# One softmax step placed elsewhere in the expert stage of a two-layer decoder trunk, with two slots for its operand

## The chip, the cores and the metric

The kernel runs on 1 core of one Trainium2 chip. The time is the device time of one execution in microseconds (us), taken as the median of several runs. All data is float32.

## What is computed

Two layers work on 256 tokens of width 1024: layer 0 mixes tokens by gated linear attention, layer 1 by a gated delta rule. After each mixer comes an expert stage ("PEER"), the part that the change touches. Each of 8 heads picks 16 experts of 16,384 for each token by a product of two key tables:

```python
v1, i1 = lax.top_k(s1, PEER_TOPK)            # s1, s2: scores of 128 keys each
v2, i2 = lax.top_k(s2, PEER_TOPK)
cand = (v1[..., :, None] + v2[..., None, :]).reshape(n_tok, PEER_HEADS, PEER_TOPK * PEER_TOPK)
sc, pos = lax.top_k(cand, PEER_TOPK)         # idx: the experts that pos stands for
gate = jax.nn.softmax(sc, axis=-1).astype(h.dtype)
...
ue = jnp.take(u, ib, axis=0)                 # a row of 1024 numbers for each chosen expert
act = gb * jax.nn.gelu(jnp.einsum('nd,nkd->nk', tb, ue))
ve = jnp.take(v, ib, axis=0)
return jnp.einsum('nk,nkd->nd', act, ve)
```

## The kernel before

The expert stage is cut into four **stretches**: layer 0 with tokens 0 to 127 and 128 to 255, then layer 1 likewise (`w` = 0 to 3 in the code, stretches 1 to 4 in the text). A stretch has four **head pairs**, so there are 16 pairs, k = 0 to 15. A pair has 32 chosen experts for each of the 128 tokens (tokens lie on the partitions). One step s of a pair takes one expert for each token.

Each engine has a program of its own, and an engine works strictly in its order. Where two programs run on one engine (experts and mixer), the generator `interleave` merges them by the due times that each `yield` names; the times are written out by hand and decide the order only. The mixer of layer 1 runs beside stretches 2 and 3.

For a pair k the work is:

- **Routing** on VectorE (DVE), `routing(k)`: top 16 of the two score lists, of the 256 sums, then the indices `idx`, in 14 slices. Slices 1 to 14 of pair k + 1 lie behind the dots 11 to 24 of pair k (s = 10 to 23). Slice 9 writes the scores less their maximum into `ex`; slice 14 writes `idx` and `spread_i`. For the first pair of stretches 1, 3 and 4 (k = 0, 8, 12) routing stands as one block ahead of the pair's dots; pair 4, the first of stretch 2, is routed in pair 3.
- **Exponential** on ScalarE (ACT), `exp(k)`, in place in `ex`, then **softmax** on VectorE, `softmax(k)`: a sum, a reciprocal and a product, three small instructions, into `gate`.
- **Gathers** by GpSimd (POOL): from s = 0 on one indirect DMA of 128 rows of `u` for each step into one of 8 buffers `ub` (line 1961), behind `idx_ready`; gather n waits until dot n - 8 has run. Beside them run the gathers of `v` rows of the pair before (line 1972), 12 buffers.
- **Dots** on VectorE (line 1129), one for each step: the product of a gathered row with the token, summed.
- **Slot rows**: TensorE (PE) transposes `spread_i` (line 1582) into PSUM; VectorE makes from it the row numbers of the `v` gathers, `slot_rows(k)`, behind the ninth dot (s = 8).
- **Weights** behind the second dot of the next pair: gelu of the dots (ACT) times `gate`, transposed by TensorE, and products with the gathered `v` rows (line 1596) into the sum `y`.

At the end of a stretch VectorE adds the gated sum `y` to `x` (lines 1110 to 1114), for which ScalarE copies the gate rows (`gate_rows`, line 1335) out of PSUM. SyncE's queue streams weight blocks of 1 MB through three ring places (line 351); the next is issued when TensorE has used the block three before.

The lines before that the text speaks of:

```python
if p == w == 0:
    yield t0 - 42
    for i, _ in enumerate(routing(k)):
        yield t0 - 40 + 2 * i
    softmax(k)
...
if s == 8:
    slot_rows(k)
if s >= 10:
    next(ahead, None)
```

Of the kernel before, what the change touches and what calls it, by code (L numbers as in the profile page):

```python
# [19 lines left out]
P = 128  # L20
# [6 lines left out]
class Signal:  # L27
# [9 lines left out]
    def next(self):  # L37
        self.base += 1
        return self.base
# [39 lines left out]
def trunk_kernel(nc, x_in, c, ada_w, ada_b, norm_mix_g, norm_ffn_g, gla_w_in, gla_g1, gla_w_g2, gla_b_g2, gla_norm_g,  # L79
# [16 lines left out]
    with ctx:  # L96
# [674 lines left out]
        def decoder(scr):  # L771
# [7 lines left out]
            NL = len(LEVELS)  # L779

# [21 lines left out]
            best, ex = sb(scr, "best", [P, 2, TOPK]), sb(scr, "ex", [P, 2, TOPK])  # L802
# [4 lines left out]
            idx, idxf = sb(scr, "idx", [P, 2, SP_], U32), sb(scr, "idxf", [P, SP_])  # L807
            gate, dots = sb(scr, "gate", [P, 2, SP_]), sb(scr, "dots", [P, 2, SP_])
            spread_i, spread_a = sb(scr, "spread_i", [P, 4, SP_]), sb(scr, "spread_a", [P, 4, SP_])
            half4 = sb(scr, "half4", [P, 2 * SP_])  # L810
            idx4 = sb(scr, "idx4", [P, 2, SP_], U32)
# [152 lines left out]
            with nc.Block() as block:  # L964
# [18 lines left out]
                def _(dve):  # L983
# [4 lines left out]
                    def routing(k):  # L988
# [65 lines left out]
                        dve.tensor_tensor(by_head(idx[:, k % 2, :]), chosen[:, :, 0, :], chosen[:, :, 1, :], ALU.add).then_inc(idx_ready.sem, 1)  # L1054
# [3 lines left out]
                        dve.tensor_tensor(spread_i[:], idxf[:].unsqueeze(1).to_broadcast([P, 4, SP_]), mask4[:], ALU.mult).then_inc(idx_spread.sem, 1)  # L1058
                        yield

                    def softmax(k):
                        dve.wait_ge(exp_done.sem, exp_done.at(k + 1))
                        link(dve.tensor_reduce(total[:], ex[:], AX, ALU.add))
                        link(dve.reciprocal(total[:], total[:]))
                        dve.tensor_tensor(gate[:, k % 2, :].rearrange("p (h n) -> p h n", n=TOPK), ex[:],
                                          total[:].unsqueeze(2).to_broadcast([P, 2, TOPK]), ALU.mult).then_inc(gates_ready.sem, 1)

                    def slot_rows(k):
                        dve.wait_ge(idx_turned.sem, idx_turned.at(k + 1))
                        pairs = turned_idx.rearrange("p (n a) -> p n a", a=2)  # L1070
                        link(dve.tensor_copy(half4[:], pairs[:, :, 0]))
                        link(dve.tensor_tensor(half4[:], half4[:], pairs[:, :, 1], ALU.add))
# [11 lines left out]
                    def experts():  # L1084
# [4 lines left out]
                        for w in range(4):  # L1089
                            layer, t = w // 2, w % 2  # L1090
                            for p in range(PAIRS + 1):
# [33 lines left out]
                                for s in range(SP_):  # L1125
# [7 lines left out]
                                    if s == 8:  # L1133
                                        slot_rows(k)
# [900 lines left out]
```

## Time and profile before

| | |
|---|---|
| median of 3 runs | 1979.09 us (1977.34 to 1979.3) |
| span of the profiled execution | 2045.4 us, mean granted clock of TensorE 0.811 |
| PE / DVE / ACT / POOL busy | 74% / 56% / 19% / 52% of the span |
| moved by DMA | 703.86 MB, mean 344 GB/s |

The profiled execution has no time of its own beside its span, which runs from its first to its last instruction and is 66 us longer than the median; everything read from the trace is on this longer scale. "Busy" counts the time in instructions; idle time is put down to whatever released the engine. The granted clock is a share of 2.4 GHz.

### The profile page before, as it was taken

Reading aid. Unit: us, or ns where it says so; the run is one execution under the profiler, and the core shown is the slowest. Engines: PE = TensorE matmul, PEld = TensorE weight load, DVE = VectorE, ACT = ScalarE, POOL = GpSimd, SP = SyncE. Lnnn points to the kernel's source line nnn. Section 1 sums busy time; section 2 is a strip of 40 time slices with the busy share of each in tenths; the row PEclk is TensorE's granted clock in tenths of the full one; section 3 lists DMA queues with packets and bytes.
Section 4 is the critical chain, followed back from the end, with each engine's and each line's share of the span. In section 5 each row is a group of like instructions: output and inputs, shape, how many; then the busy total and the mean of one; then the engine's idle time right before and its main releaser. Section 6 shows DMA issues by size and latency. Waiting matters only on the chain.

```text
span 2045.4 us, 21763 instructions
## 1 busy us (share of the span) xinstructions
PE 1518.1 (74%) x8148; PEld 975.4 (48%) x8148; DVE 1153.2 (56%) x2731; ACT 390.4 (19%) x912; POOL 1065.9 (52%) x1031
## 2 busy tenths in 40 slices
PE   7998985777788668767887866877878751656656
PEld 6743882443443556656654465665655620000001
DVE  5454386555550878567443386858734448656430
ACT  1212110000000551451211164144121110000000
POOL 0000157766655565754564456465566365666664
PEclk8999976666667879989998878989899885667678
DMA  9453499999999998897999899799799988999997
GB/s 347 177 211 149 170 390 393 410 411 412 411 411 362 376 371 299 336 393 241 346 414 412 335 391 353 245 369 389 242 393 414 412 330 312 377 370 375 375 375 268
DMA packets 173113, 703.86 MB, mean 344 GB/s; under 512 B 23360, under 2 KB 23744, under 8 KB 155728
## 3 DMA queue, kind: packets, MB, share of 16 engines
q0 software_dynamic: 147456, 536.94, 69.1%
q1 hardware_dynamic: 25552, 165.53, 20.2%
q8 instruction: 65, 1.06, 0.2%
q14 instruction: 40, 0.33, 0.0%
HBM read 701.34 MB, written 1.05 MB: 343 GB/s over the span
## 4 chain that ended last, share of the span: by engine, by line
PE 24%; POOL 16%; DVE 16%; issue 14%; DMA 11%; another core or an unknown queue 5%; ACT 4%; POOLq 0%; SPq 0%; DVEq 0%; ACTq 0%
DMA ub<-in_peer_u,idx 8%; POOL ub L1961 7%; DVE ub L1129 7%; POOL vb L1972 6%; PE PS L1596 6%; PE PS L1704 3%; PE PS L1640 2%; POOL mods L1972 2%; PE PS L1927 2%; PE PS L1878 2%; DMA ring<-in_gdn_z 2%; DVE ring L1244 1%; PE PS L1657 1%; ACT ring L1418 1%
## 5 line engine op out<-in xcount | busy, mean ns | idle before, releaser
L1961 POOL DMA_INDIRECT ub<-in_peer_u,idx x512 | 540.9, 1056 | 413.2 <-DVE dots L1129 244.6
L1129 DVE CUSTOM_DVE_ANT_0 ub<-ub,h 128x1024 f32<-128x1024 f32 x384 | 464.2, 1223 | 219.9 <-DMA ub<-in_peer_u,idx 155.2
L1596 PE MATMUL PS<-vb,z 128*32 128x512 f32 x1348 | 395.7, 774 | 110.0 <-DMA vb<-in_peer_v,idx 62.4
L1972 POOL DMA_INDIRECT vb<-in_peer_v,idx x337 | 346.5, 1028 | 198.3 <-issue 94.8
L1596 PEld LDWEIGHTS PS<-vb,z 128*32 128x32 f32 x1348 | 64.5, 126 | 333.2 <-issue 187.8
L1129 DVE CUSTOM_DVE_ANT_0 ub<-ub,PS 128x1024 f32<-128x1024 f32 x128 | 154.0, 1218 | 100.3 <-DMA ub<-in_peer_u,idx 71.7
L1657 PEld LDWEIGHTS PS<-c_act,ring 128*128 128x128 f32 x896 | 139.8, 245 | 61.3 <-issue 61.2
L1657 PE MATMUL PS<-c_act,ring 128*128 128x1 f32 x896 | 141.0, 286 | 31.9 <-issue 31.6
L1596 PE MATMUL PS<-mods,z 128*32 128x512 f32 x444 | 138.0, 782 | 34.8 <-DMA mods<-in_peer_v,idx 25.9
L1972 POOL DMA_INDIRECT mods<-in_peer_v,idx x111 | 117.8, 1061 | 33.9 <-issue 33.9
L1704 PE MATMUL PS<-hT,ring 128*128 128x128 f32 x1024 | 127.1, 286 | 7.7 <-DMA ring<-in_gdn_qkv 7.6
L1704 PEld LDWEIGHTS PS<-hT,ring 128*128 128x128 f32 x1024 | 122.9, 201 | 16.2 <-DMA ring<-in_gdn_qkv 8.9
L1972 POOL DMA_INDIRECT ub<-in_peer_v,idx x64 | 59.9, 936 | 112.3 <-DVE dots L1129 48.3
L1946 POOL IOTA iota<- 128x16 f32 x1 | 0.1, 149 | 204.9 <-POOLq L408 204.9
L1575 PE MATMUL PS<-ident,spread_a 128*128 128x128 f32 x16 | 6.0, 378 | 107.2 <-issue 67.4
L1418 ACT ACTIVATE ring<-ring,taps 128x128 f32<-128x128 f32 x256 | 76.4, 387 | 0.3
L1927 PE MATMUL PS<-hT,ring 128*128 128x128 f32 x512 | 65.6, 292 | 10.0 <-ACT z L1321 10.0
L1301 ACT ACTIVATE ex<-ex 128x32 f32<-128x32 f32 x16 | 3.7, 229 | 356.8 <-DVE ex L1038 251.7
L1927 PEld LDWEIGHTS PS<-hT,ring 128*128 128x128 f32 x512 | 63.9, 208 | 16.2 <-ACT z L1321 10.5
L1878 PE MATMUL PS<-ring,hT 128*128 128x256 f32 x256 | 60.7, 396 | 12.5 <-DMA ring<-in_gdn_z 8.2
L1596 PEld LDWEIGHTS PS<-mods,z 128*32 128x32 f32 x444 | 22.6, 126 | 99.2 <-DMA mods<-in_peer_v,idx 63.2
L1897 PE MATMUL PS<-ring 128*128 128x256 f32 x256 | 59.7, 390 | 5.4 <-DMA ring<-in_gdn_w_out 5.2
(328 smaller groups left out, 2232.9 us busy)
## 6 DMA issues: line engine op xcount, KB each, us to landing
ring<-in_gdn_qkv SPq DMA_DIRECT2D x32, 1024.0 KB
ring<-in_ada_late SPq DMA_DIRECT2D x28, 1024.0 KB
ring<-in_peer_wq SPq DMA_DIRECT2D x24, 1024.0 KB
ring<-in_ada_w SPq DMA_DIRECT2D x10, 2048.0 KB, 8.2
ring<-in_gdn_z SPq DMA_DIRECT2D x16, 1024.0 KB
ring<-in_gdn_w_out SPq DMA_DIRECT2D x16, 1024.0 KB
ring<-in_gla_w_in SPq DMA_DIRECT2D x6, 2048.0 KB, 8.3
ub<-in_peer_u,idx POOLq DMA_INDIRECT x512
```

The costliest lines, as they stand in the source:

```text
L1129: dve.tensor_tensor_reduce(out=ub[:, n % UB, :], in0=ub[:, n % UB, :], in1=by_token, scale=1.0, scalar=0.0, op0=ALU.mult, op1=ALU.add, acc ...
L1244: dve.tensor_tensor(dst[:, vs, :], dst[:, vs, :], core.ps(name, lv, gq), ALU.add).then_inc(emptied["D"].sem, 1)
L1418: last = act.activation(tapped_by[:, j, c, :], here[:, c, j:j + P], ACT.Copy, scale=taps[:, j, 16 * hf + 4 * un + c:16 * hf + 4 * un + c + 1])
L1596: last = pe.matmul(y[32 * j:32 * j + 32, e, :], z[:, j, 28 * b:28 * b + 32], rows[:, e * 512:(e + 1) * 512], start=False, stop=False, skip ...
L1640: last = pe.matmul(PS[:, 3 + b % 2, c * S:(c + 1) * S], w[:, k, c * P:(c + 1) * P], hT[:, k, :], start=(k == 0), stop=(k == KD - 1))
L1657: last = pe.matmul(PS[:, 7, cols:cols + 1], w[:, k, c * P:(c + 1) * P], c_act[:, k:k + 1], start=(k == 0), stop=(k == KD - 1))
L1704: last = pe.matmul(PS[:, 3 + un, (2 * bb + c) * P:(2 * bb + c + 1) * P], w[:, k, c * P:(c + 1) * P], hTm[:, k, :], start=(k == 0), stop=(k ...
L1878: last = pe.matmul(ps, hTm[:, k, :], w[:, k, :], start=(k == 0), stop=(k == KD - 1))
L1897: last = pe.matmul(ps, oT[:, part * KD + k, :], w[:, k, :], start=(part == k == 0), stop=(part == 1 and k == KD - 1))
L1927: last = pe.matmul(PS[:, 3 + un % 2, (2 * bb + c) * P:(2 * bb + c + 1) * P], w[:, k, c * P:(c + 1) * P], hTm[:, k, :], start=(k == 0), sto ...
L1961: pool.indirect_dma_start(ub[:, n % UB, :], None, u_rows, off).then_inc(u_land[n % UB].sem, 16)
L1972: pool.indirect_dma_start(rows, None, v_rows, off).then_inc(land.sem, 16)
```

## The change

It does four things.

1. `softmax(k)` for k = 0, 8 and 12 no longer follows that pair's routing; it stands behind the sixth dot (s = 5) of the pair itself.
2. For the other 13 pairs `softmax` no longer stands behind the last dot of the pair before (s = 31) but behind its dot 26 (s = 25); their `exp` is due at 20/32 of the pair, where it was due at 22/32.
3. `ex` and `spread_i` get two slots, taken in turn. The wait on `exp_done` ahead of writing `ex` is gone, and the wait on `idx_turned` ahead of writing `spread_i` is for one pair earlier. `softmax` also waits on `gates_ready` of the softmax before it. `half4` is no longer a tile of its own but the first 64 columns of `fold`.
4. On ScalarE `exp(8)` and `exp(12)` stand ahead of the gate rows of the stretch that ends, where they stood behind them.

```diff
+            def routed_in(w, p):
+                k = w * PAIRS + p
+                return [(k + 1, 10)] if w == 0 or p < PAIRS - 1 else []
...
-            best, ex = sb(scr, "best", [P, 2, TOPK]), sb(scr, "ex", [P, 2, TOPK])
+            best, ex = sb(scr, "best", [P, 2, TOPK]), sb(scr, "ex", [P, 2, 2, TOPK])
...
-            half4 = sb(scr, "half4", [P, 2 * SP_])
+            half4 = fold[:, 0, 0:2 * SP_]
...
-                        if k:
-                            dve.wait_ge(exp_done.sem, exp_done.at(k))
-                        dve.tensor_tensor(ex[:], best[:], best[:, :, 0:1].to_broadcast([P, 2, TOPK]), ALU.subtract).then_inc(ex_ready.sem, 1)
+                        dve.tensor_tensor(ex[:, nth_routed[k] % 2], best[:], best[:, :, 0:1].to_broadcast([P, 2, TOPK]), ALU.subtract).then_inc(ex_ready.sem, 1)
...
-                        if k:
-                            dve.wait_ge(idx_turned.sem, idx_turned.at(k))
+                        if nth_routed[k] >= 2:
+                            dve.wait_ge(idx_turned.sem, idx_turned.at(nth_routed[k] - 1))
...
                     def softmax(k):
-                        dve.wait_ge(exp_done.sem, exp_done.at(k + 1))
-                        link(dve.tensor_reduce(total[:], ex[:], AX, ALU.add))
+                        mine = ex[:, nth_routed[k] % 2]
+                        dve.wait_ge(exp_done.sem, exp_done.at(nth_routed[k] + 1))
+                        if nth_routed[k]:
+                            dve.wait_ge(gates_ready.sem, gates_ready.at(nth_routed[k]))
+                        link(dve.tensor_reduce(total[:], mine, AX, ALU.add))
...
                                     for i, _ in enumerate(routing(k)):
                                         yield t0 - 40 + 2 * i
-                                    softmax(k)
...
                                             yield ROUTE_AT[w + 1] + 2 * i + 2
-                                        softmax(k)
...
+                                late = [k] if p == 0 and w != 1 else []
...
-                                    if s == 8:
-                                        slot_rows(k)
-                                    if s >= 10:
-                                        next(ahead, None)
-                                for _ in ahead:
-                                    pass
-                                if following is not None:
-                                    softmax(following)
+                                    for j in late if s == 5 else []:
+                                        softmax(j)
+                                    for j, _, after in turned_in(w, p):
+                                        if s == after:
+                                            slot_rows(j)
+                                    for steps_of, j, first in ahead:
+                                        if first <= s < first + 14:
+                                            next(steps_of)
+                                        if s == min(first + 15, SP_ - 1):
+                                            for _ in steps_of:
+                                                pass
+                                            softmax(j)
...
-                                if p < PAIRS - 1 or (w == 0 and p == PAIRS - 1):
-                                    yield t0 + span * 22 / SP_
-                                    exp(k + 1)
+                                for j, first in routed_in(w, p) if p < PAIRS else []:
+                                    yield t0 + span * (first + 10) / SP_
+                                    exp(j)
+                                if p == PAIRS and w + 1 in ROUTE_AT:
+                                    yield ROUTE_AT[w + 1] + 21
+                                    exp(k)
                                 if p == PAIRS:
                                     yield t0 + span * 25 / SP_
                                     gate_rows((1, 3, 5, 6)[w], w % 2)
-                                if p == PAIRS and w + 1 in ROUTE_AT:
-                                    yield ROUTE_AT[w + 1] + 21
-                                    exp(k)
```

`turned_in(w, p)` gives slot rows the place that they had (s = 8), and `nth_routed[k]` is k. The orders of TensorE, GpSimd and SyncE are the same as before, instruction for instruction.

The first place is VectorE at the first pair. In the rows, `ISA ub,dots` with the `ISA dots` behind it is one dot, and `total` and `gate` are softmax. Before, behind the routing of pair 0:

```order
L1055 TENSOR_TENSOR idxf<-chosen 128x32
L1058 TENSOR_TENSOR spread_i<-idxf,mask 128x128
L1063 TENSOR_REDUCE total<-ex 128x2
L1064 RECIPROCAL total<-total 128x2
L1065 TENSOR_TENSOR gate<-ex,total 128x32
L1129 ISA ub,dots<-ub,h 128x1024
L1129 ISA dots 128x1
L1129 ISA ub,dots<-ub,h 128x1024
```

After the change, from the sixth dot of pair 0 on; the five dots ahead of it follow `spread_i` directly:

```order
L1142 ISA ub,dots<-ub,h 128x1024
L1142 ISA dots 128x1
L1078 TENSOR_REDUCE total<-ex 128x2
L1079 RECIPROCAL total<-total 128x2
L1080 TENSOR_TENSOR gate<-ex,total 128x32
L1142 ISA ub,dots<-ub,h 128x1024
L1142 ISA dots 128x1
L1142 ISA ub,dots<-ub,h 128x1024
L1142 ISA dots 128x1
L1142 ISA ub,dots<-ub,h 128x1024
L1142 ISA dots 128x1
L1086 COPY fold<-PS 128x64
```

Softmax moved over six dots; three dots are left between it and the copy that begins slot rows.

The second place is VectorE at the border of pairs 0 and 1, which stands for the 13 pairs of point 2. Before, from dot 32 of pair 0 on:

```order
L1129 ISA ub,dots<-ub,h 128x1024
L1129 ISA dots 128x1
L1063 TENSOR_REDUCE total<-ex 128x2
L1064 RECIPROCAL total<-total 128x2
L1065 TENSOR_TENSOR gate<-ex,total 128x32
L1129 ISA ub,dots<-ub,h 128x1024
L1129 ISA dots 128x1
L1129 ISA ub,dots<-ub,h 128x1024
L1129 ISA dots 128x1
L1081 TENSOR_TENSOR gate<-dots,gate 128x32
L1082 TENSOR_TENSOR spread_a<-gate,mask 128x128
```

After, from dot 26 of pair 0 on:

```order
L1142 ISA ub,dots<-ub,h 128x1024
L1142 ISA dots 128x1
L1078 TENSOR_REDUCE total<-ex 128x2
L1079 RECIPROCAL total<-total 128x2
L1080 TENSOR_TENSOR gate<-ex,total 128x32
L1142 ISA ub,dots<-ub,h 128x1024
L1142 ISA dots 128x1
```

The three instructions of softmax stand six dots earlier, and dot 32 is followed by the next pair's dots.

The third place is ScalarE at the border of stretches 2 and 3, where `h<-PS` is the copy of the gate rows and `mods<-PS` the last two copies of scores. Before:

```order
L1528 ACTIVATE mods<-PS 128x512 x2
L1335 ACTIVATE h<-PS 128x1024
L1301 ACT_TABLE_LOAD
L1301 ACTIVATE ex<-ex 128x32
L1372 ACT_TABLE_LOAD
L1372 ACTIVATE nrs<-eps 128x1
```

After:

```order
L1546 ACTIVATE mods<-PS 128x512 x2
L1319 ACT_TABLE_LOAD
L1319 ACTIVATE ex<-ex 128x32
L1353 ACTIVATE h<-PS 128x1024
L1390 ACT_TABLE_LOAD
L1390 ACTIVATE nrs<-eps 128x1
```

The exponential and its table load moved ahead of the gate rows; the number of table loads is the same.

## Rows read from the trace of the kernel before

**Rows 1.** The page: part 1 by engine, and the DMA line of part 2 (40 slices).
```profile
PE 1518.1 (74%) x8148; PEld 975.4 (48%) x8148; DVE 1153.2 (56%) x2731; ACT 390.4 (19%) x912; POOL 1065.9 (52%) x1031
...
DMA  9453499999999998897999899799799988999997
```

**Rows 2.** One source line, L1063: count, durations, and what ended its waits.
```profile
L1063 DVE TENSOR_REDUCE total<-ex x16: 174/180/188, 256.5 to 1896.2; 128x2 f32<-128x32 f32 x16
...
  issue: 47.7, 2
  ACT ex L1301: 15.3, 1
```

**Rows 3.** Timeline of VectorE, first pair: start, duration, instruction, [idle before <- releaser].
```profile
240.93 0.29 DVE L1058 TENSOR_TENSOR spread_i<-idxf,mask 128x128 f32<-128x128 f32 x1
...
256.49 0.19 DVE L1063 TENSOR_REDUCE total<-ex 128x2 f32<-128x32 f32 x1 [15.27 <-ACT ex L1301]
...
257.02 1.22 DVE L1129 CUSTOM_DVE_ANT_0 ub<-ub,h 128x1024 f32<-128x1024 f32 x1
...
266.19 1.22 DVE L1129 CUSTOM_DVE_ANT_0 ub<-ub,h 128x1024 f32<-128x1024 f32 x1
...
271.88 0.22 DVE L1071 COPY half<-PS 128x64 f32<-128x64 f32 x1 [4.46 <-issue]
```

**Rows 4.** Timeline of TensorE at the end of the first score products.
```profile
269.72 2.01 PE L1630 MATMUL PS<-keysT,ring 128*128 128x128 f32 x16
271.57 0.27 PE L1582 MATMUL PS<-ident,spread_i 128*128 128x128 f32 x1
```

**Rows 5.** Timeline of GpSimd: gathers of key rows, first pair.
```profile
241.08 1.10 POOL L1961 DMA_INDIRECT ub<-in_peer_u,idx  x1 [34.75 <-DVE idx L1054]
...
258.52 1.68 POOL L1961 DMA_INDIRECT ub<-in_peer_u,idx  x1 [7.65 <-DVE dots L1129]
...
272.34 0.94 POOL L1961 DMA_INDIRECT ub<-in_peer_u,idx  x1 [0.30 <-issue]
```

**Rows 6.** Timeline of SyncE's queue: weight blocks, first pair.
```profile
238.72 8.13 SPq L351 DMA_DIRECT2D ring<-in_peer_wq  x2
254.32 47.58 SPq L351 DMA_DIRECT2D ring<-in_ada_late  x8
```

**Rows 7.** Busy time by stretch: PE, PEld, DVE, ACT, POOL, granted clock, DMA share, GB/s.
```profile
240.00:272.00 32.00, 32.00 (x172) 28.74 (x170) 12.10 (x27) 6.92 (x16) 19.01 (x16) 1.00 0.95 342
272.00:316.00 44.00, 29.54 (x158) 29.45 (x157) 43.18 (x115) 2.27 (x6) 26.07 (x24) 0.55 1.01 410
316.00:640.00 324.00, 245.42 (x1136) 130.29 (x1137) 164.47 (x404) 10.18 (x16) 216.45 (x212) 0.65 1.02 407
```

**Rows 8.** Timeline of VectorE at the border of stretches 2 and 3.
```profile
1161.49 0.19 DVE L1063 TENSOR_REDUCE total<-ex 128x2 f32<-128x32 f32 x1 [23.83 <-issue]
...
1166.51 0.69 DVE L1110 TENSOR_TENSOR h<-PS,h 128x512 f32<-128x512 f32 x1 [4.41 <-PE PS L1562]
...
1182.92 0.18 DVE L1162 TENSOR_TENSOR xa<-ab,dtb 128x16 f32<-128x16 f32 x1 [3.52 <-ACT ab L1382]
```

**Rows 9.** Timeline of ScalarE at the same border.
```profile
1152.85 0.60 ACT L1528 ACTIVATE mods<-PS 128x512 f32<-128x512 f32 x1 [0.85 <-remote]
1158.90 1.02 ACT L1335 ACTIVATE h<-PS 128x1024 f32<-128x1024 f32 x1 [5.45 <-PE PS L1610]
...
1161.23 0.23 ACT L1301 ACTIVATE ex<-ex 128x32 f32<-128x32 f32 x1
```

**Rows 10.** Timeline of ScalarE in stretch 3: one exponential behind the mixer's work.
```profile
1336.15 0.22 ACT L1301 ACTIVATE ex<-ex 128x32 f32<-128x32 f32 x1
```

**Rows 11.** Timeline of VectorE in stretch 3: the 27th dot of that pair, and the wait after dot 28.
```profile
1340.93 1.22 DVE L1129 CUSTOM_DVE_ANT_0 ub<-ub,h 128x1024 f32<-128x1024 f32 x1
...
1348.82 0.69 DVE L1184 TENSOR_TENSOR ring<-ring 128x512 f32<-128x512 f32 x1 [5.51 <-issue]
```

**Rows 12.** One source line, L1961: gathers of key rows, durations min/median/max.
```profile
L1961 POOL DMA_INDIRECT ub<-in_peer_u,idx x512: 932/937/1989, 241.1 to 1978.2; - x171
```

More of the change, by code:

```diff
@@ L779, in decoder, with turned_in @@
             NL = len(LEVELS)
+            IDX, IDX4 = 2, 2
+            ROUTED = list(range(4 * PAIRS))
+            nth_routed = {k: n for n, k in enumerate(ROUTED)}
+            def turned_in(w, p):
+                return [(w * PAIRS + p, 3, 8)]
+            def routed_in(w, p):
+                k = w * PAIRS + p
+                return [(k + 1, 10)] if w == 0 or p < PAIRS - 1 else []
             area = ring_flat[:, 3 * 2048:]
@@ L1073, in slot_rows @@
-                        quads = half4[:].rearrange("p (n a) -> p n a", a=2)
-                        dve.tensor_tensor(idx4[:, k % 2, :], quads[:, :, 0], quads[:, :, 1], ALU.add).then_inc(rows_ready.sem, 1)
+                        link(dve.tensor_copy(half4, pairs[:, :, 0]))
+                        link(dve.tensor_tensor(half4, half4, pairs[:, :, 1], ALU.add))
+                        quads = half4.rearrange("p (n a) -> p n a", a=2)
+                        dve.tensor_tensor(idx4[:, k % IDX4, :], quads[:, :, 0], quads[:, :, 1], ALU.add).then_inc(rows_ready.sem, 1)
@@ L1084, in experts @@
+                        dve.tensor_tensor(spread_a[:], gate[:, k % IDX, :].unsqueeze(1).to_broadcast([P, 4, SP_]), mask4[:], ALU.mult).then_inc(acts_ready.sem, 1)
                     def experts():
@@ L1115, in experts @@
                                     break
-                                following = k + 1 if p < PAIRS - 1 or w == 0 else None
-                                ahead = routing(following) if following is not None else iter(())
+                                ahead = [(routing(j), j, first) for j, first in routed_in(w, p)]
+                                late = [k] if p == 0 and w != 1 else []
                                 if layer and p == 0:
@@ L1566, in experts @@
                         pe.wait_ge(prepared.sem, prepared.at(1))
+                        turns = 0
                         for w in range(4):
@@ L1590, in experts @@
                                         yield t0 + span * (4 * b + 4) / SP_
+                                        if turning and turning[0][1] <= 4 * b + 4:
+                                            turning, turns = turn_rows()
                                         for e in range(2):
@@ L1606, in experts @@
                                             spread_gate(GATE_FFN[w // 2])
+                                while turning:
+                                    yield t0 + span * turning[0][1] / SP_
+                                    turning, turns = turn_rows()
                     def spread_gate(q):
```

54 lines of the change are left out of this document (29 added, 25 removed).

## Prediction

> **What bounds the kernel now.** I read the page first. No engine is busy all the time, but the DMA line stands at 9 tenths through most of the span [rows 1]. The table by stretch then says who rules at the place that the change touches: from 240 to 272 us TensorE is busy in all 32.00 us (the score products of layer 0), from 272 to 316 VectorE is busy in 43.18 of 44, and from 316 to 640 the DMA share is 1.02 at 407 GB/s while VectorE works 164 of 324 us [rows 7]. So stretch 1 is bound by TensorE, then VectorE, then DMA. Last I took the waits of softmax itself: 16 softmaxes, 15.3 us of wait for the exponential once, and 47.7 us in two others [rows 2]. All the rest ran without a wait. The change can only gain at these three places, and each must be followed to the next wait.
>
> **The start of stretch 1 (k = 0).** VectorE ends the routing with `spread_i` at 240.93 and stands until 256.49, since ScalarE does the exponential between copies that wait for score products; the first dot begins at 257.02 [rows 3]. The first gather was issued at 241.08 [rows 5]. The trace doesn't show how soon its row could be used. Bounds: not before the 1.10 us of the issue itself, and not later than the 7.67 us from the issue of gather 9 at 258.52 to the ninth dot at 266.19 [rows 3, 5]. I take the upper end, 248.8 us for the first dot, since it is a real row under load. The first six dots take 6 x 1.15 = 6.9 us (nine dots run from 257.02 to 267.4) and end at about 255.7. Softmax then waits for the same exponential, about 0.8 us, and ends at 257.0; dots 7 to 9 run until 260.5, where they ended at 267.4. That is 6.9 us ahead.
>
> What is late next is slot rows. Before, VectorE had run its nine dots and waited 4.46 us more, until 271.88 [rows 3]. That wait ends with TensorE's transpose at 271.57, which stands behind the last score products at 269.72 [rows 4]. TensorE has no gap there [rows 7], its order is unchanged, and nothing on VectorE feeds it. So the wait grows from 4.46 to 11.3 us, and dot 10 starts when it did. **Term 1: 0 us on VectorE.**
>
> What remains is that gathers move forward. Gathers 9 to 17 (n = 8 to 16) wait for dots 1 to 9, and were issued from 258.52 to 272.34 [rows 5]; now they are out by about 262. How far DMA was behind at 272: issued were the 16 gathers of the window at 0.524 MB, 8.4 MB, and 5 blocks of 1.05 MB (2 and the first 3 of 8), 5.2 MB [rows 6, 7]; moved were 342 GB/s x 32 us = 10.9 MB. So 2.7 MB, 6.5 us of DMA, were outstanding, and most of that is done earlier now. From 272 to 316 VectorE alone sets the pace: 23 more gathers (24 in the window, one begun before it) and 5 blocks are 17.3 MB against 410 x 44 = 18.0 moved, which leaves 2.0 MB, 4.8 us, at 316 [rows 7]. Only what is left then can shorten the stretch bound by DMA that follows. Bounds: 0 us and -4.8 us. Rows in flight are never zero, and while VectorE sets the pace a shorter queue only lets DMA idle, so I take a third. **Term 2: -1.5 us.**
>
> One rule would lower even this. The Trainium skill, SBUF — State Buffer, "SBUF: two separate sides", says that a VectorE instruction with two SBUF inputs and GpSimd share a pair of ports exclusively, so that descriptors from GpSimd wait. The trace agrees: 1.68 us at 258.52, with dots running, and up to 1.989 against a median of 0.937 [rows 5, 12]. Two gathers more than before now run under dots; by these rows each is up to 1.05 us longer, 2 us in all, and the last still ends 8 us before 271.88. By the rule as by the rows the sum stays.
>
> **The borders of stretches 2/3 and 3/4 (k = 8, 12).** Softmax at 1161.49 ended a wait of 23.83 us, but the next instruction waits again, 4.41 us, until 1166.51, for the closing product of the values [rows 8]. Without softmax the engine waits for that alone. On ScalarE the exponential moves from 1161.23 to behind the score copy that ends at 1153.45; VectorE had finished that routing by 1137.7 (1161.49 - 23.83) [rows 8], and a wait of 5.45 us follows, which holds the 1.28 us table load and 0.23 us of work (together 1.5); the gate copy starts at 1158.90 as before [rows 9]. Softmax reappears behind dot 6, in front of a wait of 3.52 us [rows 8]. The other border has the same form. **Term 3: 0 us.**
>
> **The 13 other pairs.** Softmax moves from dot 32 to dot 26. It costs 0.53 us (256.49 to 257.02) [rows 3]. New waits: it needs the exponential six dots earlier. I matched all 13; the smallest distance is at k = 10, exponential at 1336.15 and 27th dot at 1340.93, 4.8 us, so none waits [rows 10, 11]. Behind it are six dots; their buffers come free 0.53 us later, and the gathers and weights that wait for them too. After dot 32 the same 0.53 us falls away. At k = 10 VectorE waits 5.51 us after dot 28 [rows 11], so it lands in a hole. Where VectorE is never idle between the two places the sum is zero by the next pair's first dot. **Term 4: 0 us**, with bounds of -0.53 and +0.53 for each pair, 6.9 us for all.
>
> **Slots and waits.** The waits taken away were met before: each is implied by a softmax or slot-row wait that VectorE had passed. The new wait on `gates_ready` is for its own earlier instruction. `half4` in `fold` costs nothing, since `fold` is used only in slices 11 to 13 of routing. **Term 5: 0 us.**
>
> Sum: 0 - 1.5 + 0 + 0 + 0. The terms come from an execution whose span is 2045.4 us, 3.4% over the median of 1979.09; scaling them changes less than 0.1 us. Forecast: 1977.5 us. A difference of 0.2%, 4 us, is about what can be told from no change.
>
> **The rivals.**
> - *The start gains in full* (0.07). If the transpose were not the next wait, the first dot's gain, 257.02 - 248.8 = 8.2 us, would pass through: 1971. For it: the 15.27 us wait is the longest that the change removes [rows 3]. Against it: the wait at 271.88 [rows 3, 4].
> - *The queue is worth more* (0.18). If nearly all of the 4.8 us of outstanding transfers at 316 turns into time, and some of the pair ends pay 0.53 us, the time is about 1974 to 1972. For it: DMA at 1.02 from 316 to 640 [rows 7].
> - *Softmax behind dot 26 delays the loop* (0.11). Its place falls where VectorE is catching up after routing, and buffers come free late; behind dot 32 it fell into a wait for rows. If all 13 pay 0.53 us: 1979.1 + 6.9 = 1986. It decides when GpSimd waits for dots 27 to 32 with DMA idle; against it, DMA has transfers queued in stretch 1 [rows 7], and at k = 10 a hole follows [rows 11].
> - *No change within 0.2%, as forecast* (0.64).
>
> **Numbers.** Faster by over 0.2%: 0.07 + 0.18 = 0.25, and the forecast case keeps 0.64. Slower 0.11. The forecast's own range is 1975.1 to 1981; to hold 8 in 10 it reaches down to the second rival, 1971.5, and up a part of the way into the third, to 1983.
>
> **What would show it.** In the changed trace the first dot starts near 249 us or before it, the wait ahead of the copy in slot rows grows from 4.46 to about 11 us, and that copy still starts near 271.9 behind the transpose. The DMA outstanding at 272 shrinks. At the two borders the first residual multiply still waits for the closing product, now some 29 us in one piece. No softmax behind a dot 26 waits. The prediction is wrong if the slot-row copy starts several us earlier, if stretch 1 ends over 4 us earlier though it doesn't, or if GpSimd's waits for dots grow by several us in pairs 1 to 15.

## The result, and the profile after

The changed kernel takes 1983.88 us (median of 20 runs, 1977.23 to 1991.43) against 1979.98 us for the kernel before (20 runs, 1977.34 to 1984.16). The ratio is 1.0018, 95% interval 1.0009 to 1.0026; the means are 1983.59 and 1980.28, 3.3 us apart. So no gain came, and a small loss is more likely than none: 1983.88 lies 0.9 us above my range and 6.4 us above my forecast. (Of the 6.4 us, 0.9 are the base: I had taken 1979.09 us for the kernel before.)

To read the numbers one has to know that chips differ here. The profile of before [rows 1 to 12], with a span of 2045.4 us, looks like those of chips on which that kernel takes some 2050 us, while its median of 1979 and the whole result above are like those of chips on which it takes about 3.4% less. That this one profile came from such a chip is inferred, from its span and from its waits, shown further below. If it is so, the gap that I had put beside the span was the chip's.

Lines of the page of the changed kernel: span, busy time by engine, the DMA line, and the two costliest groups (engine or group, busy us, count or mean; last the idle time ahead and what ended it):

```profile
span 1975.2 us, 21762 instructions
...
PE 1531.1 (78%) x8148; PEld 966.6 (49%) x8148; DVE 1154.8 (58%) x2731; ACT 389.9 (20%) x912; POOL 1075.4 (54%) x1031
...
DMA  8463399999999999799899999999899998999997
...
L1993 POOL DMA_INDIRECT ub<-in_peer_u,idx x512 | 538.8, 1052 | 447.1 <-DVE dots L1142 266.5
L1142 DVE CUSTOM_DVE_ANT_0 ub<-ub,h 128x1024 f32<-128x1024 f32 x384 | 465.0, 1222 | 294.5 <-DMA ub<-in_peer_u,idx 293.1
```

Busy times are within 1% of those of before [rows 1]: nothing was added or taken away. GpSimd still waits mostly for dots (266.5 us) and VectorE for rows (293.1 us), so the expert loop is a circle of gather, landing and dot. The start of stretch 1 on VectorE, in the timeline (start, duration, engine, line, operation, and the idle time ahead with its releaser):

```profile
240.42 0.29 DVE L1070 TENSOR_TENSOR spread_i<-idxf,mask 128x128 f32<-128x128 f32 x1
...
245.03 1.23 DVE L1142 CUSTOM_DVE_ANT_0 ub<-ub,h 128x1024 f32<-128x1024 f32 x1 [4.32 <-DMA ub<-in_peer_u,idx]
...
252.81 1.22 DVE L1142 CUSTOM_DVE_ANT_0 ub<-ub,h 128x1024 f32<-128x1024 f32 x1 [2.15 <-DMA ub<-in_peer_u,idx]
...
257.88 0.18 DVE L1078 TENSOR_REDUCE total<-ex 128x2 f32<-128x32 f32 x1
...
263.05 1.23 DVE L1142 CUSTOM_DVE_ANT_0 ub<-ub,h 128x1024 f32<-128x1024 f32 x1
...
271.37 0.23 DVE L1086 COPY fold<-PS 128x64 f32<-128x64 f32 x1 [7.08 <-PE PS L1604]
```

The first dot starts 12 us earlier than before (245.03; 257.02 in [rows 3]), softmax waits for nothing behind dot 6, and the ninth dot starts at 263.05 instead of 266.19. Then the copy of the slot rows waits 7.08 us for TensorE and starts at 271.37, where it started at 271.88 before. The 12 us are gone at that place; that they would be was forecast. All 16 softmaxes of the changed kernel run without any wait; one line's view of the sum in softmax says so, with nothing behind the word "until":

```profile
L1078 DVE TENSOR_REDUCE total<-ex x16: 175/180/183, 257.9 to 1823.4; 128x2 f32<-128x32 f32 x16
its engine sat idle before it (us, times) until:
```

### The profile page after: what moved, and what is told of

Same layout as the page of the kernel before. It is cut to its first block, busy times and chain, and to the rows that moved or that the text cites. A ratio compares the mean times of both kernels' runs of the same rounds, so it can differ in the third digit from the quotient of the medians.

```text
span 1975.2 us, 21762 instructions
## 1 busy us (share of the span) xinstructions
PE 1531.1 (78%) x8148; PEld 966.6 (49%) x8148; DVE 1154.8 (58%) x2731; ACT 389.9 (20%) x912; POOL 1075.4 (54%) x1031
## 3 DMA queue, kind: packets, MB, share of 16 engines
q0 software_dynamic: 147456, 536.94, 70.6%
## 4 chain that ended last, share of the span: by engine, by line
DMA 26%; POOL 19%; PE 19%; DVE 14%; issue 9%; ACT 2%; POOLq 0%; DVEq 0%; ACTq 0%
DMA ub<-in_peer_u,idx 17%; POOL ub L1993 8%; POOL vb L2004 7%; DVE ub L1142 6%; PE PS L1625 3%; DMA vb<-in_peer_v,idx 3%; DMA ub<-in_peer_v,idx 3%; PE PS L1672 3%; POOL mods L2004 2%; POOL ub L2004 2%; PE PS L1959 2%; DMA ring<-in_gdn_z 2%; PE PS L1910 1%; PE PS L1831 1%; DVE ring L1261 1%
## 5 line engine op out<-in xcount | busy, mean ns | idle before, releaser
L1993 POOL DMA_INDIRECT ub<-in_peer_u,idx x512 | 538.8, 1052 | 447.1 <-DVE dots L1142 266.5
L1142 DVE CUSTOM_DVE_ANT_0 ub<-ub,h 128x1024 f32<-128x1024 f32 x384 | 465.0, 1222 | 294.5 <-DMA ub<-in_peer_u,idx 293.1
L1625 PE MATMUL PS<-vb,z 128*32 128x512 f32 x1348 | 411.9, 774 | 104.9 <-DMA vb<-in_peer_v,idx 101.4
L2004 POOL DMA_INDIRECT vb<-in_peer_v,idx x337 | 355.4, 1055 | 117.1 <-issue 100.1
L1625 PE MATMUL PS<-mods,z 128*32 128x512 f32 x444 | 147.0, 800 | 45.7 <-DMA mods<-in_peer_v,idx 45.5
L1736 PE MATMUL PS<-hT,ring 128*128 128x128 f32 x1024 | 124.2, 284 | 3.2 <-DMA ring<-in_gdn_qkv 3.2
L1736 PEld LDWEIGHTS PS<-hT,ring 128*128 128x128 f32 x1024 | 121.0, 199 | 10.9 <-issue 6.7
L1625 PE MATMUL PS<-ub,z 128*32 128x512 f32 x256 | 68.3, 627 | 10.5 <-DMA ub<-in_peer_v,idx 10.4
L1959 PEld LDWEIGHTS PS<-hT,ring 128*128 128x128 f32 x512 | 60.1, 197 | 7.1 <-issue 5.0
L1959 PE MATMUL PS<-hT,ring 128*128 128x128 f32 x512 | 61.8, 282 | 1.6 <-ACT z L1339 1.6
```

The lines of the kernel that those rows point to most:

```text
L1142: dve.tensor_tensor_reduce(out=ub[:, n % UB, :], in0=ub[:, n % UB, :], in1=by_token, scale=1.0, scalar=0.0, op0=ALU.mult, op1=ALU.add, acc ...
L1625: last = pe.matmul(y[32 * j:32 * j + 32, e, :], z[:, j, 28 * b:28 * b + 32], rows[:, e * 512:(e + 1) * 512], start=False, stop=False, skip ...
L1736: last = pe.matmul(PS[:, 3 + un, (2 * bb + c) * P:(2 * bb + c + 1) * P], w[:, k, c * P:(c + 1) * P], hTm[:, k, :], start=(k == 0), stop=(k ...
L1959: last = pe.matmul(PS[:, 3 + un % 2, (2 * bb + c) * P:(2 * bb + c + 1) * P], w[:, k, c * P:(c + 1) * P], hTm[:, k, :], start=(k == 0), sto ...
L1993: pool.indirect_dma_start(ub[:, n % UB, :], None, u_rows, off).then_inc(u_land[n % UB].sem, 16)
L2004: pool.indirect_dma_start(rows, None, v_rows, off).then_inc(land.sem, 16)
```

## The experiments

Each experiment ran beside the kernel before on its own chip. Its ratio is to that. The first three sets, of four each, ran on three chips of the slower sort (before: 2052.05, 2052.26 and 2061.69 us), the last two sets (`e13` to `e16`, `e17` and `e18`) on two chips of the faster sort (1982.74 and 1980.99 us). Each chip was used for one set. This turned out to matter.

### The parts one by one, slower chips

`e1`: the kernel before with the start alone; softmax of pair 0 stands behind its sixth dot and no longer ahead of the dots.

```diff
-    softmax(k)
...
+    if s == 5 and k == 0:
+        softmax(k)
```

> The kernel before with one move: softmax of pair 0 from behind its routing to behind its sixth dot. Theory S (the start pays): the changed kernel's first dot came at 245.03 us and six dots waited for rows in between, gathers and weight blocks of the first 30 us were packed closer, and the order in which transfers of stretch 1 are served shifts; then this kernel alone is slower than before by 2 to 4 us. Theory E (the pair ends pay): within 1 us of before. Theory L (layout and slots pay): within 1 us. My own forecast (a shorter DMA queue at 316 us) would be 1.5 us faster.

Measured: 2058.74 us, ratio 1.0030 [1.0005, 1.0054].

`e2`: the 13 pair ends alone; the last two lines are the due time of the exponential on ScalarE.

```diff
-for _ in ahead:
-    pass
-if following is not None:
-    softmax(following)
+    if s == 25 and following is not None:
+        softmax(following)
...
-yield t0 + span * 22 / SP_
+yield t0 + span * 20 / SP_
```

> The kernel before with the softmax of 13 pairs behind dot 26 in place of dot 32, and their exponential due at 20/32. Theory E: each pair's last six dots free their buffers 0.53 us later while VectorE catches up, of which half returns; slower by 2 to 5 us, and GpSimd's waits for dots grow. Theories S and L: within 1 us of before.

Measured: 2058.18 us, 1.0029 [1.0004, 1.0054].

`e3`: the two borders alone (softmax of k = 8 and 12 behind the sixth dot, the exponential ahead of the gate rows).

> The kernel before with softmax of pairs 8 and 12 behind their sixth dots and their exponentials ahead of the gate rows. All theories so far: within 1 us of before, since the next instruction of VectorE waits for the closing product anyway. If the 0.53 us in front of the mixer's first steps in stretch 3 counts, or the copy of the gate rows comes late, slower by 1 to 2 us.

Measured: 2054.22 us, 1.0014 [0.9994, 1.0034].

`e4`: the two slots, the waits and `half4` in `fold` alone, every softmax at its old place.

> The changed kernel with every softmax and exponential back at its old place, so that only the two slots, the waits and the shared tile for the halves differ from before; the instruction orders are those of before. Theory L: slower by 2 to 4 us. Theories S and E: within 1 us of before.

Measured: 2050.3 us, 1.0003 [0.9981, 1.0024]. The slots cost nothing that can be told.

On the next chip, from the other side: `e5` is the changed kernel itself, `e6` the changed kernel with the start put back, `e7` with the ends put back, `e8` the kernel before as a control.

> The changed kernel itself, as the sum beside which its parts are read. All theories: slower than before by 0.1 to 0.5%.

> The changed kernel with only the softmax of pair 0 back ahead of the first dot. Theory S (the start pays most): within 0.1% of before. Theory E (the pair ends pay most): as slow as the changed kernel. If both pay alike, as the first four runs suggest (1.0030 and 1.0029), half of the changed kernel's excess is left.

> The changed kernel with only the softmax of the 13 pairs back behind dot 32 and their exponentials at 22/32. Theory E: within 0.1% of before. Theory S: as slow as the changed kernel. If both pay alike: half of the excess is left.

> The kernel before, submitted as if it were an experiment, to see what the comparison gives for no change and to have its trace from the same chip. All theories: ratio 1.000, inside its interval; if it comes out near 1.002, the earlier ratios of the parts say little.

Measured: e5 1.0040 [1.0013, 1.0067], e6 1.0034 [1.0007, 1.0061], e7 1.0013 [0.9991, 1.0036], e8 1.0021 [0.9998, 1.0044]. The control shows how little one such comparison can carry: the same kernel, 0.2% apart. A least-squares fit over the 166 single runs of these eight and of before gives the ends +4.5 us (95%: 2.1 to 6.8) and the start +2.8 us (0.5 to 5.2), with nothing for borders and slots; if every experiment is allowed a common offset, which the control suggests, 3.4 us (0.8 to 6.0) and 1.8 us (-0.8 to 4.4). At this point the pair ends looked like the cause.

### Work behind dot 26 and behind dot 32, a third slower chip

`e9`: the softmaxes behind dot 26 with the exponentials left where they were; `e10`: the reverse.

> The kernel before with its 13 softmaxes of a pair end behind dot 26, the exponentials left at their old due time (22 of 32). Theory E (the softmax and its wait for the exponential, taken behind dot 26, hold up the dots, the release of row buffers and so the queue): as the run that moved both, ratio 1.002 to 1.004 (plus 4 us), since both parts' place on VectorE is the same. Rival X (it is the place of the exponential on ScalarE that costs): ratio 1.000 to 1.001. Rival N (nothing of the ends costs, the differences so far are noise): 1.000 plus or minus 0.001.

> The kernel before with only the due time of the exponential in ScalarE's order at 20 of 32 in place of 22; the softmax stays behind dot 32. On ScalarE it changes the place of two exponentials by two rows each. Theory E: ratio 1.000 plus or minus 0.001. Rival X: 1.002 to 1.004.

Measured: e9 2071.87 us, 1.0067 [1.0035, 1.0098]; e10 2067.85 us, 1.0020 [0.9988, 1.0052]. The place on ScalarE by itself shows no cost that can be told from none. e9 is dearer than e2, whose VectorE program is the same; no softmax behind a dot 26 waits in its trace, so I have no cause for that surplus.

`e11` and `e12`: more work of the same kind, in two places, in `e11` under `if s == 25:`, in `e12` behind the last dot.

```diff
+for _ in range(4 if following is not None else 0):
+    link(dve.tensor_reduce(total[:], best[:], AX, ALU.add))
+    link(dve.reciprocal(total[:], total[:]))
```

> The kernel before with four more reductions and reciprocals (their results unused) behind dot 26 of each of the 13 pairs whose end is followed by a softmax: about 1.7 us of VectorE work each, 21 us in all, that is three times the work that the change moves there. If a delay of the dots at dot 26 costs in full: plus 21 us (ratio 1.010). Theory E (about plus 4 us for 13 times 0.53 = 6.9 us, 0.6 of it): plus 13 us or more, and more than the same work behind dot 32. Rival N: as much as behind dot 32, within 2 us.

> The same four reductions and reciprocals, 21 us in all, behind dot 32, ahead of the softmax at its old place. If work at the pair's end is in the shadow of the gathers of the next pair: plus 0 to 5 us. Theory E: less by at least 5 us than the same work behind dot 26. Rival N: the same as behind dot 26 within 2 us, whatever its size.

Measured: e11 2072.58 us, 1.0063 [1.0034, 1.0092]; e12 2064.74 us, 1.0010 [0.9983, 1.0037]. The same 21 us of VectorE work cost 11.9 us behind dot 26 and nothing that can be told behind dot 32 (differences of the means: +11.9 and -0.1 us). The 12.0 us between the two are three times what the control showed between two equal kernels, so for this chip the place matters; but its single runs scatter widely (`e12`: 2047 to 2070 us), and e11 has only seven. The traces of the slower chips also differ in kind. The sum in softmax of the control again, which answers to [rows 2], and the same line of `e14` below, whose softmaxes wait at the same three places, on the faster chip:

```profile
L1063 DVE TENSOR_REDUCE total<-ex x16: 175/182/186, 259.3 to 1903.6; 128x2 f32<-128x32 f32 x16
...
  issue: 49.9, 2
  ACT ex L1301: 15.3, 1
```

```profile
L1063 DVE TENSOR_REDUCE total<-ex x16: 178/181/186, 256.9 to 1823.4; 128x2 f32<-128x32 f32 x16
...
  ACT ex L1299: 70.6, 3
```

All three waits have a releaser on the faster chip; on the slower one two don't. That doesn't mean that nothing ended them: in the profile of before the exponential ends at 1161.46, and the softmax that waited for it starts 0.03 us later [rows 8, 9]. In e9 I count 38 waits of VectorE over 2 us for which the timeline names no work of another engine and no transfer; in the changed kernel's trace, and in each of e13 to e18, there is one, of 3.0 us. How many of the 38 are ordinary waits without a name is open. They stand elsewhere in each kernel, so I lay no single slow trace beside another.

### The ends again, faster chip

`e14` is e2 once more; `e13` has the softmax behind dot 30; `e15` is e11 with sixteen rounds in place of four; `e16`, shown here, has every softmax, that of the start and of the borders too, behind the sixth dot of its own pair.

```diff
-    softmax(k)
...
+    if s == 5:
+        softmax(k)
...
-if following is not None:
-    softmax(following)
```

> The kernel before with the 13 softmaxes of a pair end behind dot 30 (exponential due at 20 of 32, as in the run behind dot 26). Theory E (what lies inside the stretch of dots costs by how far it stands from the pair's end): between the two places, ratio 1.000 to 1.002, and at least 2 us below the same edit behind dot 26. Rival P (any place off the pair's end costs the same): the same as behind dot 26 within 1.5 us.

> The 13 softmaxes behind dot 26 and nothing else, a second time, beside the run behind dot 30. Theory E and rival P: ratio 1.002 to 1.004. Rival N (nothing of the ends costs): 1.000 plus or minus 0.001.

> Sixteen more reductions and reciprocals behind dot 26 of the 13 pairs in place of four: about 6.6 us each, 86 us in all. If the dots' delay costs in proportion, by the run with four (11 us for 21): plus 45 us (ratio 1.022). If the row buffers cover a part of each delay and only what exceeds it costs: more than proportional, plus 60 us or more. If the landings of rows bound the loop and VectorE catches up: plus 25 us or less.

> The kernel before with every softmax, that of the first pair and of the borders too, behind the sixth dot of its own pair; the exponentials left where they are, so that none is waited for. Theory E (only the last dots of a pair are sensitive): ratio 0.998 to 1.0005. Rival P (the softmax costs at any place inside the dots, by its length): 1.002 to 1.004, as behind dot 26.

Measured: e13 1.0010 [0.9993, 1.0027], e14 0.9993 [0.9978, 1.0007], e15 1.0096 [1.0074, 1.0119], e16 1.0032 [1.0018, 1.0047]. Of what theory E expected only the ratio of e13 came: behind dot 26 the ends cost nothing that can be told (e14), so nothing was left for dot 30 to lie below, and a softmax near the pair's start, which should have been free, costs. e15 shows how much of such work is covered by waits that are there anyway: 86 us of additional work cost 17.9 us (means), 0.21 for 1. By that ratio the 6.9 us of the 13 softmaxes would be worth 1.4 us at most.

### The start again, faster chip

`e17` is e1 once more, `e18` is e6 (the whole change, start put back).

> The start alone (first pair's softmax behind its sixth dot, exponential where it was), a second time. Theory S (the dots that begin 12 us earlier set off row gathers that disturb what streams beside them, and more is lost by the fourth pair than the start gains): ratio 1.0015 to 1.003. Rival R (the start costs nothing by itself; what costs is the sum of small delays of all softmaxes inside the dots): 0.999 to 1.001.

> The changed kernel with the first pair's softmax back ahead of its dots, a second time. Theory S: 0.999 to 1.001. Rival R: 1.0015 to 1.003, like the changed kernel.

Measured: e17 1983.59 us, 1.0014 [1.0000, 1.0028]; e18 1981.83 us, 1.0002 [0.9989, 1.0015]. Doing the start alone brings +3.1 us in the means (e17), undoing it leaves +0.3 (e18), the full change has +3.3. The fit over the 128 single runs of the result, e14, e17, e18 and their runs of before: start +3.2 us (95%: 1.7 to 4.6), ends -0.1 us (-1.3 to 1.1). It takes borders and slots as nothing (with a term for them the start is 3.0, 1.5 to 4.5) and the single runs as independent; no unchanged control ran on these chips. With that said, on the chips on which the result was measured, the start is the cause.

### Where the start loses

The traces of the faster chips can be laid side by side. Busy time by stretch (length, PE, PEld, DVE, ACT, POOL, granted clock, DMA share, GB/s), the changed kernel, then e14, in which the start is as before, then e17, the start alone:

```profile
240.00:272.00 32.00, 32.00 (x174) 28.82 (x172) 12.67 (x29) 7.16 (x17) 20.88 (x17) 1.00 0.99 383
272.00:316.00 44.00, 29.09 (x154) 29.00 (x153) 43.09 (x115) 1.76 (x4) 26.21 (x20) 0.54 0.98 378
316.00:366.00 50.00, 42.77 (x170) 23.61 (x170) 26.16 (x73) 1.56 (x2) 38.71 (x38) 0.58 1.00 387
366.00:415.00 49.00, 37.26 (x157) 16.21 (x157) 27.45 (x60) 1.74 (x3) 37.77 (x37) 0.69 1.02 411
```

```profile
240.00:272.00 32.00, 32.00 (x169) 28.70 (x168) 12.35 (x26) 7.08 (x16) 18.62 (x16) 1.00 0.93 339
272.00:316.00 44.00, 29.43 (x163) 29.34 (x160) 42.97 (x115) 2.50 (x6) 26.36 (x23) 0.56 1.02 411
316.00:366.00 50.00, 41.02 (x199) 19.68 (x200) 27.79 (x78) 1.56 (x2) 38.11 (x40) 0.70 1.02 409
366.00:415.00 49.00, 34.50 (x135) 12.03 (x133) 27.98 (x60) 1.74 (x3) 36.26 (x36) 0.72 1.02 411
```

```profile
240.00:272.00 32.00, 32.00 (x170) 28.72 (x170) 12.86 (x26) 6.93 (x17) 19.57 (x17) 1.00 0.98 376
272.00:316.00 44.00, 29.70 (x161) 29.61 (x159) 43.25 (x115) 2.46 (x6) 25.50 (x20) 0.55 0.98 381
316.00:366.00 50.00, 40.61 (x158) 22.36 (x162) 25.38 (x73) 1.56 (x2) 39.33 (x36) 0.57 0.98 377
```

Until 272 the early start moves more (383 against 339 GB/s). After that it moves less, though nothing on VectorE is later. ("The queue" is here what has been issued and not yet been moved.) Up to 366 us the changed kernel moved 383 x 32 + 378 x 44 + 387 x 50 = 48.2 MB, e14 moved 49.4 MB; 1.14 MB at 411 GB/s are 2.8 us. Its 65th dot starts 2.9 us later (415.27 against 412.33). For e17 the same sum gives 47.6 MB, 4.2 us, and its 65th dot stands at 416.63, 4.3 us later.

The first dots of the two traces lie apart by other things too: e14's routing ends 0.9 us later. Counted from the routing's end (`spread_i`), the 65th dots are 3.8 and 4.5 us apart, so bytes and times agree to about 1 us.

Closer, the same view from 304 to 328 us, the changed kernel and e14:

```profile
304.00:312.00 8.00, 0.00 (x0) 0.00 (x0) 7.86 (x20) 0.00 (x0) 5.49 (x4) 0.50 0.99 384
312.00:320.00 8.00, 1.98 (x4) 1.12 (x5) 5.23 (x12) 1.79 (x3) 6.66 (x5) 0.50 0.80 253
320.00:328.00 8.00, 6.74 (x26) 1.77 (x24) 3.68 (x6) 0.00 (x0) 6.17 (x7) 0.78 0.96 349
```

```profile
304.00:312.00 8.00, 0.00 (x0) 0.00 (x0) 7.86 (x20) 0.00 (x0) 4.77 (x4) 0.50 1.02 412
312.00:320.00 8.00, 0.15 (x1) 0.15 (x1) 6.39 (x12) 0.23 (x1) 6.17 (x7) 0.50 1.01 393
320.00:328.00 8.00, 7.59 (x35) 3.13 (x35) 3.70 (x6) 1.56 (x2) 5.94 (x7) 0.68 1.01 406
```

From 312 to 320 the DMA engines of the changed kernel are at 0.80 and move 253 GB/s. The queue has run empty. Why it isn't refilled, the timeline of GpSimd shows, first the changed kernel, then e14:

```profile
308.17 1.36 POOL L2004 DMA_INDIRECT vb<-in_peer_v,idx  x1 [0.30 <-issue]
309.83 1.99 POOL L1993 DMA_INDIRECT ub<-in_peer_u,idx  x1 [0.30 <-issue]
312.12 1.99 POOL L2004 DMA_INDIRECT vb<-in_peer_v,idx  x1 [0.30 <-issue]
314.42 1.98 POOL L1993 DMA_INDIRECT ub<-in_peer_u,idx  x1 [0.30 <-issue]
316.70 1.22 POOL L2004 DMA_INDIRECT vb<-in_peer_v,idx  x1 [0.31 <-issue]
```

```profile
309.07 1.36 POOL L1970 DMA_INDIRECT vb<-in_peer_v,idx  x1 [0.31 <-issue]
310.73 1.99 POOL L1959 DMA_INDIRECT ub<-in_peer_u,idx  x1 [0.30 <-issue]
313.02 0.93 POOL L1970 DMA_INDIRECT vb<-in_peer_v,idx  x1 [0.30 <-issue]
314.26 0.93 POOL L1959 DMA_INDIRECT ub<-in_peer_u,idx  x1 [0.30 <-issue]
315.50 0.94 POOL L1970 DMA_INDIRECT vb<-in_peer_v,idx  x1 [0.30 <-issue]
```

GpSimd waits for nothing in either, so the length of its instruction sets the supply: with 1.99 us and the 0.30 between two, 0.524 MB every 2.3 us, 229 GB/s; with 0.94 us, 0.524 MB every 1.24 us, 423 GB/s. VectorE tells the two apart. The dots of the changed kernel and those of e14 at that time:

```profile
312.08 1.22 DVE L1142 CUSTOM_DVE_ANT_0 ub<-ub,h 128x1024 f32<-128x1024 f32 x1
...
313.23 1.22 DVE L1142 CUSTOM_DVE_ANT_0 ub<-ub,h 128x1024 f32<-128x1024 f32 x1
...
314.37 1.22 DVE L1142 CUSTOM_DVE_ANT_0 ub<-ub,h 128x1024 f32<-128x1024 f32 x1
```

```profile
313.06 1.23 DVE L1129 CUSTOM_DVE_ANT_0 ub<-ub,h 128x1024 f32<-128x1024 f32 x1
...
314.33 1.22 DVE L1129 CUSTOM_DVE_ANT_0 ub<-ub,h 128x1024 f32<-128x1024 f32 x1
...
315.60 1.23 DVE L1129 CUSTOM_DVE_ANT_0 ub<-ub,h 128x1024 f32<-128x1024 f32 x1
```

These are dots 31 to 33, in both. In the changed kernel they start 1.15 us apart, the pace of dots without a gap, and their rows have landed: the trace's DMA records have the row of dot 32 at 311.97, 1.25 us ahead of it. In e14 they start 1.27 us apart, each some 0.12 us later than it could: the rows of dots 31 and 33 land at 313.04 and 315.58, 0.02 us ahead of their dots. Where the dots run without a gap, GpSimd needs 1.99 us; where each leaves a small one, 0.93 us. So a long queue protects itself: it makes the dots wait, and the waits let GpSimd issue. A short one lets the dots run closed, and GpSimd falls behind just when the queue needs it.

That it is the dots' second input that stretches the gathers, and not something else about that time, stretch 4 shows. There the dots take the token from PSUM, TensorE's output memory (`ub,PS`), and no longer from SBUF, the memory of the rows (`ub,h`). The same place of a pair in the changed kernel, GpSimd and then VectorE:

```profile
1671.22 0.93 POOL L1993 DMA_INDIRECT ub<-in_peer_u,idx  x1 [0.30 <-issue]
1672.46 0.94 POOL L2004 DMA_INDIRECT vb<-in_peer_v,idx  x1 [0.31 <-issue]
```

```profile
1671.83 1.21 DVE L1142 CUSTOM_DVE_ANT_0 ub<-ub,PS 128x1024 f32<-128x1024 f32 x1
...
1672.97 1.21 DVE L1142 CUSTOM_DVE_ANT_0 ub<-ub,PS 128x1024 f32<-128x1024 f32 x1
```

These dots run without a gap, 1.14 us apart, and the gathers are short. In the six traces of the changed kernel, e13, e14, e16, e17 and e18, 36 gathers began amid dots of this kind that follow each other within 1.16 us: each took 0.93 or 0.94 us. Amid such dots with the token in SBUF there were 62: 1.17 to 1.99 us, the median 1.98.

The other traces of the faster chips agree in the main (e15 is left out, since its additional work lies in this very place). Counted from the start of `spread_i`, from 67 to 77 us GpSimd starts 5 gathers in the changed kernel, e17 and e16 (the early starts) and 7, 7 and 6 in e14, e18 and e13 (start as before). From 312 to 320 us the first three move 253, 265 and 262 GB/s, the other three 393, 405 and 398. The 65th dot stands at 174.9, 175.5 and 174.8 us behind `spread_i` in the first three, at 171.0, 171.4 and 173.2 in the others, 3.2 us apart in the mean, as much as the start's +3.2 us of the fit. e13 is the worst of its group, and has a dip of its own, 325 GB/s, from 320 to 328. The early part of the slower traces says the same: 5 gathers and a 65th dot at 175.8 to 177.0 us in e1, e5 and e7; 6 or 7 gathers and 171.4 to 174.5 us in before, e2, e3, e4, e6, e8 and e10. Only e9, at 176.4 with 7 gathers, doesn't fit; e11 and e12, like e15, add work in this place.

## Why the prediction was wrong

**Term 1, the start on VectorE (0 us).** Right in mechanism and size. Of the signs I had named, the first dot came at 245.03 (I had 248.8), the copy still started behind the transpose, at 271.37, and its wait grew, to 7.08 us instead of 11.3: six of the first nine dots waited for rows, 9.8 us in all before dots 1 to 5 and 2.15 before the eighth, so that the nine were some 3 us ahead and not 6.9. That VectorE gained nothing was right.

**Term 2, the queue (-1.5 us).** This is the step that failed, and it failed in sign. My text said that "while VectorE sets the pace a shorter queue only lets DMA idle, so I take a third". I let it idle between 272 and 316 at no price, since all of its backlog would be done earlier, and set the bounds at 0 and -4.8 us, none of them a loss. The runs show +3.2 us (1.7 to 4.6) for the start: against e14 the changed kernel moved 1.4 MB more until 272, and 2.1 MB less from 296 to 366. In the same part I weighed the rule that decides it. I counted only the two gathers that newly ran under the first nine dots, 2 us in all, and left out what an emptier queue does at dots 29 to 33: it lets them follow each other without a gap, and then a gather takes 1.99 instead of 0.94 us. The Trainium skill, SBUF — State Buffer, "SBUF: two separate sides", says that a VectorE instruction with two SBUF inputs and a GpSimd instruction that reads SBUF exclude each other from a shared pair of ports. The trace agrees: 1.99 us with both inputs of the dots in SBUF, 0.94 us with one in PSUM. What is shown: that the start costs the time, that the DMA engines stand at 0.80 there, and that gathers are long amid gapless dots with two SBUF inputs and short amid such dots with one input in PSUM. That these few long gathers are the whole of the 3.2 us is argued from the bytes; no run kept the early start and took them away.

**Term 3, the borders (0 us).** e3 gives 1.0014 [0.9994, 1.0034], which can't be told from nothing. No run on a faster chip took them alone. The sign that I had named came: the first residual multiply waits for the closing product in one piece, 36.11 and 31.37 us (I had some 29).

**Term 4, the 13 pair ends (0 us, bounds of 6.9 either way).** On the faster chips right: -0.1 us (-1.3 to 1.1). On the slower ones the fit gives 3.4 to 4.5 us, about half of rival 3's price or more (softmax behind dot 26 delays the loop), and three times the work, added in the same place, costs 11.9 us there but none that can be told behind dot 32. Whether waits like the one that I named behind dot 28 cover it on the faster chips is not shown; e15 only shows that much is covered.

**Term 5, slots and waits (0 us).** Nothing speaks against it: e4 1.0003 [0.9981, 1.0024], on a slower chip.

**Rival 1, the start in full,** and **rival 2, the queue worth more,** both fell. What happened was none of my cases: a loss at the start, through the queue. As no case had a loss there, the slower side had only 0.11, all of it for the pair ends. Rival 2's figure was also wrong in itself: 4.8 us off 1979.1 is 1974.3, and pair ends that pay 0.53 us each, as in rival 3, raise it; 1972 needs them to gain. The lower end of my range, 1971.5, rests on it.

**The signs.** None of the three that I had named as proof against me came: the copy started at 271.37, stretch 1 ended no earlier (dot 129 is 3.7 us later than in e14, counted from `spread_i`), and GpSimd's waits for dots in the gathers of `u` are 266.5 us against 264.5 in e14. I had no sign for the step that failed. What DMA moves from 316 to 366, where I had it pace the loop, would have been one: 387 GB/s against 409 in e14.

**The base.** I put the 3.4% between span and median aside. Most of my rows stood up on the faster chip, and the two waits that end on "issue", 47.7 us together [rows 2], which I had read as waits for the exponential, have its name there (70.6 us in three with the first).

Left open: how the 3 us that the start loses by the 65th dot come through to the end. They do in the medians. In the traces, counted from `spread_i`, the three early starts are in the mean behind the three others by 3.2 us at dot 65, 3.3 at dot 129, 4.2 at dot 257, 1.7 at dot 385 and 2.0 at the last. But single traces move by as much: e14's last dot lies 0.1 us before that of the changed kernel, whose profiled execution was the fastest of its 20, e18's 6.4 us behind, and runs of one kernel scatter with a standard deviation of 3 us. Open too is why e16, with the other softmaxes near the pair's start as well, costs 6.0 us (means), 3 more than the start alone, and why e9 costs more than e2. No version here can be told to beat the kernel before; on the faster chips e14 (0.9993) and e18 (1.0002) can't be told from it.

## What to carry to other kernels

Where a loop is bound by transfers and these are issued by an engine that computing can slow, a backlog in the queue can be worth something: before counting "the queue is shorter" as a gain, ask whether it will run empty, and at what rate the issuing engine could refill it just then. Give the bound of such a term both signs. For a difference of 0.2%, do the part alone and undo it in the whole, on the same sort of chip as the result, beside an unchanged control.

## What the runs showed of the hardware

On one and the same kernel the faster chips took 3.4 to 4% less time (1980 to 1983 us against 2052 to 2062). As each chip was used once, that it is the chip and not the hour is inferred. The granted clock is only a little lower on the slower ones (mean 0.808 in the control, 0.826 in the changed kernel). What stands out is what the DMA engines move late in the kernel. The control and the changed kernel in stretch 4, which takes the control some 319 us from its first to its last dot and the changed kernel 299:

```profile
1700.00:1900.00 200.00, 108.50 (x253) 17.11 (x254) 131.73 (x322) 8.12 (x12) 130.51 (x137) 0.69 0.95 359
```

```profile
1700.00:1900.00 200.00, 129.29 (x312) 19.77 (x310) 125.25 (x295) 5.32 (x9) 151.20 (x160) 0.73 1.03 409
```

It is alike in e5 and e9 (355 and 359 GB/s) and in e14 and e17 (409). Why is open; so is what the 38 waits without a name in e9 are. The same edit may have another price on the two sorts: the pair ends +4.5 us (2.1 to 6.8) on the one, -0.1 us (-1.3 to 1.1) on the other, but with the common offset allowed the first interval begins at 0.8 and the two overlap.

The instruction with which GpSimd issues a gather took 0.93 to 0.94 us in the undisturbed case, and 1.17 to 1.99 us amid gapless dots with both inputs in SBUF (62 gathers). With one input of the dots in PSUM (36 gathers), and in e14 with gaps of 0.12 us between them (three), it took 0.93 to 0.94 us.
